# Values beside scores, a bank emptied ahead of a branch's end, and a gate product ahead of a scaling, in a three-block float32 transformer kernel

## The reference, cut to what matters

```
x = first_block(x, ...)     # two layers, each a mixer and a SwiGLU of width 2816
                            #   layer 0: short convolution and multiscale pooling
                            #   layer 1 ("block 1" below): sparse attention (8 heads of 64, 2 key groups;
                            #            selected + window + compressed branch) beside a 31-tap convolution
x = second_block(x, ...)    # "block 2"

# second_block
hn   = rms_norm(x)
qa,ka,va,ga, qb,kb,vb,gb, qc,kc,vc,gc, gate_logits = split(hn @ w_in)
o_a  = moba_attention(norm(qa), norm(ka), va)            # 8 heads
o_b  = dilated_attention(norm(qb), norm(kb), vb)         # 3 groups of 8 heads, merged by their log-sums
o_c  = swa_sink_attention(norm(qc), norm(kc), vc, sinks) # 8 heads, 2 key heads
branches = [o_a * silu(ga), o_b * silu(gb), o_c * silu(gc)]
br   = branches[i] @ w_branch[i]                         # i = 0, 1, 2
merged = sum(sigmoid(gate_logits[i]) * br[i])
x = x + merged @ w_out
```

## Time and profile before

| | |
|---|---|
| median of 3 runs | 994.49 us (994.39, 994.49, 996.18) |
| profiled execution | 996.31 us |
| its span, first to last instruction | 994.4 us |
| mean granted TensorE clock | 0.993 |
| TensorE busy | 972.7 us, 98% |
| VectorE busy | 608.2 us, 61% |
| ScalarE busy | 484.9 us, 49% |
| GpSimd busy | 213.2 us, 21% |
| HBM | 169 GB/s over the span |

### The profile page before, as it was taken

One profiled execution on the slowest core, in us unless ns is written; L12 is line 12 of the kernel. 1 busy time (PEld: TensorE's weight loads), 2 busy tenths in 40 slices (PEclk: granted clock), 3 DMA queues, 4 the chain that ended last, 5 costly groups with the idle time before them and its releaser, 6 DMA issues.

```text
span 994.4 us, 17117 instructions
## 1 busy us (share of the span) xinstructions
PE 972.7 (98%) x7057; PEld 867.0 (87%) x7057; DVE 608.2 (61%) x827; ACT 484.9 (49%) x726; POOL 213.2 (21%) x178
## 2 busy tenths in 40 slices
PE   9999999999998988999999999999999999999998
PEld 8989999999887877799999997887787888999996
DVE  5866554545488788665444446756464745856654
ACT  5446434343445364753343436456455545647451
POOL 0005970000032140000000000313543604920100
PEclk9999999999999999999999999999999999999999
DMA  8664656555557421356565663645354535553361
GB/s 267 219 217 143 216 175 205 170 199 180 179 158 238 134 99 44 127 180 202 171 208 169 204 218 128 212 169 170 127 170 165 174 129 170 170 189 111 127 211 43
DMA packets 119636, 168.75 MB, mean 170 GB/s; under 512 B 5556, under 2 KB 88596, under 8 KB 119572
## 3 DMA queue, kind: packets, MB, share of 16 engines
q1 hardware_dynamic: 118992, 167.55, 50.8%
q10 hardware_dynamic: 580, 0.30, 0.1%
HBM read 165.38 MB, written 2.46 MB: 169 GB/s over the span
## 4 chain that ended last, share of the span: by engine, by line
PE 84%; DVE 7%; ACT 3%; POOL 2%; issue 2%; SPq 1%; DMA 1%; DVEq 0%; ACTq 0%; POOLq 0%
PE ps L465 24%; PE ps L466 24%; PE ps L467 24%; PE ps L847 2%; DVE scratch_sb L1459 2%; PE ps L874 2%; PE ps L861 2%; DVE wlo_sb L445 1%; SPq L1268 1%; POOL b_inv_sb L2403 1%; PE ps L518 1%; PE ps L687 1%; PE ps L2027 1%; ACT whi_sb L422 1%; DVE nmax_sb L943 1%
## 5 line engine op out<-in xcount | busy, mean ns | idle before, releaser
L445 DVE TENSOR_TENSOR wlo_sb<-raw_sb,whi_sb 128x2048 fp32r<-128x2048 f32 x143 | 331.8, 2322 | 210.5 <-ACT whi_sb L422 210.2
L422 ACT ACTIVATE whi_sb<-raw_sb 128x2048 fp32r<-128x2048 f32 x143 | 273.8, 1916 | 186.2 <-PE ps L467 163.2
L465 PE MATMUL ps<-hhi_sb,whi_sb 128*128 128x256 f32 x1008 | 282.8, 281 | 1.7 <-ACT scratch_sb L2154 1.3
L467 PE MATMUL ps<-hhi_sb,wlo_sb 128*128 128x256 f32 x1008 | 281.4, 279 | 0.0
L466 PE MATMUL ps<-hlo_sb,whi_sb 128*128 128x256 f32 x1008 | 281.3, 279 | 0.0
L465 PEld LDWEIGHTS ps<-hhi_sb,whi_sb 128*128 128x128 f32 x1008 | 189.5, 188 | 4.1 <-issue 2.7
L466 PEld LDWEIGHTS ps<-hlo_sb,whi_sb 128*128 128x128 f32 x1008 | 189.4, 188 | 0.9
L467 PEld LDWEIGHTS ps<-hhi_sb,wlo_sb 128*128 128x128 f32 x1008 | 189.4, 188 | 0.0
L465 PE MATMUL ps<-whi_sb,hhi_sb 128*128 128x512 f32 (+2 forms) x304 | 121.1, 398 | 0.9 <-DVE wlo_sb L445 0.9
L466 PE MATMUL ps<-wlo_sb,hhi_sb 128*128 128x512 f32 (+2 forms) x304 | 117.9, 388 | 0.0
L467 PE MATMUL ps<-whi_sb,hlo_sb 128*128 128x512 f32 (+2 forms) x304 | 117.8, 388 | 0.0
(11 more groups left out here) (333 smaller groups left out, 1349.7 us busy)
## 6 DMA issues: line engine op xcount, KB each, us to landing
raw_sb<-w_in SPq DMA_DIRECT2D x45, 1024.0 KB, 5.0
raw_sb<-ffn_gate SPq DMA_DIRECT2D x22, 1024.0 KB, 5.1
raw_sb<-ffn_up SPq DMA_DIRECT2D x22, 1024.0 KB, 5.1
raw_sb<-ffn_down SPq DMA_DIRECT2D x22, 1024.0 KB, 4.8
raw_sb<-w_in_even SPq DMA_DIRECT2D x8, 1024.0 KB, 9.2
raw_sb<-w_in_odd SPq DMA_DIRECT2D x8, 1024.0 KB, 5.2
raw_sb<-w_branch SPq DMA_DIRECT2D x6, 1024.0 KB, 4.9
scratch_sb<-bias_rows_dram SPq DMA_DIRECT2D x40, 128.0 KB, 3.0
```

What stands on the lines that cost most here:

```text
L422: nc.scalar.activation(place(whi, n0), in_raw(n0), ACT.Copy).then_inc(hi_ready, 1)
L445: nc.vector.tensor_tensor(place(wlo, n0), in_raw(n0), place(whi, n0).bitcast(F32), ALU.subtract).then_inc(lo_ready, 1)
L465: nc.tensor.matmul(dst, l_hi, r_hi, start=first, stop=False)
L467: return nc.tensor.matmul(dst, l_lo, r_hi, start=False, stop=last)
```

## The change

It has five edits, all of them of order; no operation is added or removed.

- In block 2's `pe_step` the value products of the pairs before stand ahead of this step's transposes.
- In block 1 `VALUE_STEP` is 4, 8, ..., 32 instead of 6, 10, ..., 30, 32. Within a step TensorE's order is scores, transposes, values, so a value product now follows the scores of its step.
- In the segment of unit 3 the entry `finish` of branch 1 is taken out and put in behind the next `half`, which is the first half of the SiLU gate item of branch 2. On ScalarE the split of tile 34 and the emptying of that half come ahead of the exponential.
- VectorE's split of tile 46 (it stood behind the second part of tile 44, item R of branch 1) moves into `merge` (1, 1), behind its product.
- `scale_tile` of branch 2 for the first token half moves from the end of `finish2` to the same place: merge product, scaling and gating, split of tile 46, and only then the addition.

```diff
--- before.py
+++ after.py
@@ -965,12 +965,12 @@
             if 2 * m + 2 < len(jobs) // 2:
                 pair_s(pe, jobs, p0, 2 * m + 2)
                 pair_s(pe, jobs, p0, 2 * m + 3)
+            if m >= 1:
+                pair_pv(pe, jobs, p0, 2 * m - 2)
+                pair_pv(pe, jobs, p0, 2 * m - 1)
             if 0 <= 2 * m < len(jobs) // 2:
                 pair_t(pe, jobs, p0, 2 * m)
                 pair_t(pe, jobs, p0, 2 * m + 1)
-            if m >= 1:
-                pair_pv(pe, jobs, p0, 2 * m - 2)
-                pair_pv(pe, jobs, p0, 2 * m - 1)
 
         def dve_step(dve, jobs, p0, m):
             if 2 * m + 2 < len(jobs) // 2:
@@ -1011,7 +1011,7 @@
         GROUP_STEP, CONV3_REST, LATE_STEP = (10, 18, 26), 30, (10, 12, 14)
         STEPS1, FOUR_STEP = range(-2, 33), [-2, 0, 4, 8, 12, 16, 20, 24, 28, 32]
 
-        TURN_STEP, VALUE_STEP = range(1, 30, 4), [*range(6, 31, 4), 32]
+        TURN_STEP, VALUE_STEP = range(1, 30, 4), range(4, 33, 4)
 
         CONV3_AT = [0, 2, 4, 6, 8, 10, 12, 14, 16, 18, 20, 22, 25, 28, 31]
 
@@ -1924,6 +1924,9 @@
                         done = max(done, min(want, len(steps)))
                 assert done == len(steps)
                 body = mixed
+                if u == 3:
+                    k = body.index(("finish", 1))
+                    body.insert(next(j for j in range(k, len(body)) if body[j][0] == "half"), body.pop(k))
             if not order:
 
                 body[1], body[2] = body[2], body[1]
@@ -2232,7 +2235,8 @@
         def blk2_dve(dve):
             for e in order:
                 if e[0] == "weights" and e[4] == 1:
-                    split_lo(dve, e[2] + 2)
+                    if e[1][:3] != ("R", 1, 1):
+                        split_lo(dve, e[2] + 2)
                 elif e[0] == "sums":
                     _, item, nq = e
                     heads = 4 if item[0] == "kv" else 8
@@ -2276,6 +2280,9 @@
                             dve.wait_ge(b_T, LAST_Q_T)
                         nc.vector.scalar_tensor_tensor(mt[:, :, :], gs[:, :, :], 1.0, rb[:, :, :],
                                                        ALU.add, ALU.mult).then_inc(m_mul, 1)
+                        if (who, j) == (1, 1):
+                            scale_tile(dve, nc.vector, 2, 0, o_scaled, 0, FACTORS[2])
+                            split_lo(dve, n0 + 2)
                         dve.wait_ge(m_mul, 2 * who + j + 1)
                         nc.vector.tensor_tensor(macc[:, 4 * j:4 * j + 4, :], macc[:, 4 * j:4 * j + 4, :],
                                                 mt[:, :, :], ALU.add).then_inc(m_sum, 1)
@@ -2357,8 +2364,6 @@
                 step(nc.vector.tensor_tensor(comb[:, 3], comb[:, 3], comb[:, 2], ALU.add))
                 step(nc.vector.reciprocal(comb[:, 4], comb[:, 3]))
                 step(nc.vector.tensor_tensor(comb[:, 5], comb[:, 4], comb[:, 1], ALU.mult))
-            if b == 2:
-                scale_tile(dve, nc.vector, b, 0, o_scaled, 0, at)
 
 
         FACTORS = (2, 10, 17)
```

## The result

The changed kernel took 987.38 us (median of four executions, 986.99 to 989.07), the kernel before beside it 995.01 us (four, 994.39 to 996.18). The ratio is 0.9922, with a 95% interval of 0.9904 to 0.9939. It was run twice more, each time beside the kernel before: 990.25 us against 994.27 (ratio 0.9952, 0.9935 to 0.9968), and 988.04 against 994.44 (0.9932, 0.9915 to 0.9948). The three gains are 7.6, 4.0 and 6.4 us: each is clear of its interval, and the size differs. Both facts have to be explained.

A forecast was written before the change was run, and what follows sets the result against it. TensorE, busy 98% of the span, bounds the kernel; only its idle gaps, clock and gaps between instructions can give time. Terms -0.8 + 0.5 - 0.2 - 0.6 = -1.1 us take 994.49 to 993.4 us, range 989.7 to 995.8.

The forecast's parts named there:

- Part 2: Block 2's pe_step, value products ahead of transposes: a cost of 0.5 us, with the 1.89 us GpSimd wait staying.
- The same 0.08 us is a cost of each of the 15 steps: Block 2 steps holding both kinds: value products start later behind weights than transposes do, costing 0.4 to 1.2 us.
- which leaves 0.06. So this wait stays.: VectorE's copy at 693.17 comes only 0.06 us earlier, so TensorE's 1.89 us wait for GpSimd at 705.06 remains.
- Rival 1: Wait at 705.06 (1.89 us) and slow stretch behind it (1.7) go if sums come over 0.12 earlier: 989.8 us; chance 0.13.
- I cost this at nothing: Block 2, VectorE's score shifts (L886) come 0.6 or 1.1 us later in steps 1 and 2: no cost.
- rival 3: Block 2, turn of q2 at 737.92: a 1.5 us wait and a 1.7 us slow stretch, 996.6 us; chance 0.10.
- three signs of being wrong: Slow stretches other than four, GpSimd scalings changing length anywhere, or gaps around moved products not 0.1 us.
- Part 1: Block 1, values two steps earlier: output rows start sooner, gain 0.8 us, between 0.3 and 1.1.
- The delays ahead of it: Block 1, VectorE's chain held back by earlier value products: some 0.1 us, plus 0 to 0.5 us.
- Part 3: Block 2, finish 1 behind the next half: TensorE starts at 851.7 instead of 851.91, gain 0.2 us (0 to 0.4).
- Part 4: Branch 2's product at 940.36, gate product first on VectorE: gain 0.6 us of the 1.27 us wait.
- The slow stretches: TensorE at 1.2 GHz: four stretches of about 3.4 us in the trace, each costing at most 1.7 us.

The follow-up runs named there:

- e5: Kernel before, with value products ahead of transposes only in steps m = 1 and 2 of each block 2 attention unit: 994.82 us, ratio 0.9997.
- e2: Kernel before, with only block 1's VALUE_STEP changed to 4, 8, ..., 32: 993.49 us, ratio 0.9987.
- e3: Changed kernel with block 2's value-product order and block 1's VALUE_STEP turned back, leaving the finish move and the branch 2 edits: 993.22 us, ratio 0.9989.
- e4: Kernel before, with one added wait that sends VectorE's split of tile 15 behind GpSimd's scalings: 991.54 us, ratio 0.9971.
- e6: Kernel before, with value products ahead of transposes in one step alone, m = 3 of block 2's first unit: 991.38 us, ratio 0.997.
- f7: Changed kernel with transposes ahead of value products again in the third unit's step m = 2 alone: 988.43 us, ratio 0.9935.
- f9: Changed kernel with finish of branch 1 back ahead of the next half: 989.65 us, ratio 0.9953.
- h1: Changed kernel with finish of branch 1 back ahead of the half, and transposes first again in the fourth unit's step m = 2: 989.90 us, ratio 0.9951.
- a4: The whole changed kernel unaltered, run a third time beside the kernel before: 988.04 us against 994.44, ratio 0.9932.
- e1: Kernel before, with only block 2's value products put ahead of transposes in pe_step: 990.68 us, ratio 0.9965.
- f8: Changed kernel with block 1's VALUE_STEP as before: 990.33 us, ratio 0.9954.

## Why the prediction was wrong, by its own steps

**Part 2 is where it failed**, in two steps.

The first is "The same 0.08 us is a cost of each of the 15 steps". I had compared how late the first instruction of either kind starts behind weights, and left out what stands *between* the two kinds. Behind scores both kinds start alike. The timeline of before, in the first unit's m = 1, then the one of after:

```profile
677.48 0.28 PE L847 MATMUL ps<-qkh_sb,qkl_sb 64*128 64x128 f32 x2
677.70 1.09 PE L861 MATMUL ps<-ident_sb,scratch_sb 128*128 128x128 f32 x8
678.72 0.69 PE L874 MATMUL ps<-scratch_sb 128*64 128x64 f32 x16
```

```profile
674.14 0.28 PE L847 MATMUL ps<-qkh_sb,qkl_sb 64*128 64x128 f32 x2
674.36 0.69 PE L874 MATMUL ps<-scratch_sb 128*64 128x64 f32 x16
674.97 1.09 PE L861 MATMUL ps<-ident_sb,scratch_sb 128*128 128x128 f32 x8
```

The weight loads (engine PEld) that follow the eight transposes, in before and then in after:

```profile
678.72 0.55 PEld L874 LDWEIGHTS ps<-scratch_sb 128*64 128x64 f32 x16 [0.17 <-issue]
```

```profile
675.79 0.19 PEld L465 LDWEIGHTS ps<-whi_sb,hhi_sb 128*128 128x128 f32 x1
```

Eight transposes followed by value products take 678.72 - 677.70 = 1.02 us. Followed by weights they take less: 675.79 - 674.97 = 0.82 us. The value products take 0.61 us whichever comes next. So a value product behind transposes costs 0.20 us more than the next product's weights do, and the new order has no such pair. By the starts of the products themselves it is 0.17 us: the first weight product starts 0.85 us behind the transposes. The trace of before had it as an idle 0.17 us of the weight load ahead of these value products, which I did not read. Ten steps gain 0.2 each, as e5's lead shows one by one. The five steps without scores gain almost nothing (first unit: 2.34 us between the same two weight products, against 2.38).

The second is "which leaves 0.06. So this wait stays." Both numbers of that comparison were off. First the shift. VectorE's copy starts at 689.28:

```profile
689.28 1.29 DVE L894 COPY scratch_sb<-ps 128x512 f32<-128x512 f32 x2 [1.91 <-PE ps L861]
```

With the lead of 3.76 at that place this is 693.04 on the clock of before, where the copy stood at 693.17. That is 0.13 us earlier, not 0.06. I had started the sum from 691.80, the start that the chain of waits gives for the transposes; in the timeline they start at 691.64:

```profile
691.64 1.03 PE L861 MATMUL ps<-ident_sb,scratch_sb 128*128 128x128 f32 x8
```

The same sum from 691.64, with the 0.08 in it, gives 692.95, which is 0.22 us earlier. Two views differ by more than the margin that the sum was to decide.

Then the margin. I had it at 0.12 us (700.89 and 1.04 for the first scaling). The second scaling has its own row in the trace of before, and its start is 0.08 us behind the split's 701.81:

```profile
701.89 3.11 POOL L2411 TENSOR_TENSOR scratch_sb<-scratch_sb,b_inv_sb 128x512 f32<-128x512 f32 x1
```

In the changed kernel GpSimd's scalings go through (both, and then the second by itself), and VectorE's split behind them:

```profile
697.00 2.05 POOL L2416 TENSOR_TENSOR scratch_sb<-scratch_sb,b_inv_sb 128x512 f32<-128x512 f32 x2
```

```profile
698.00 1.04 POOL L2416 TENSOR_TENSOR scratch_sb<-scratch_sb,b_inv_sb 128x512 f32<-128x512 f32 x1
```

```profile
698.01 3.18 DVE L445 TENSOR_TENSOR wlo_sb<-raw_sb,whi_sb 128x2048 fp32r<-128x2048 f32 x1
```

Against the lead the scaling came 0.11 us earlier and the split 0.02, so the distance between them moved by 0.09 us, and 0.08 was enough. The second scaling now starts 0.01 us ahead of the split. All fourteen profiles follow this order of starts. In the four with the wait (before, e2, e3, e5) the split starts 0.07 to 0.08 us ahead and the second scaling takes 3.1 us. In nine of the others the scaling starts ahead by 0.02 us or less and takes 1.04; in e4 the added wait puts the split 1.13 us behind. The Trainium skill (SBUF — State Buffer, "Who interferes with whom") says that a VectorE instruction with two SBUF inputs and a GpSimd instruction that reads SBUF exclude each other for a whole instruction. The traces agree in both orders: scalings 4.12 us and split 2.29 before, 2.05 and 3.18 after.

**Rival 1 came true**, at a chance of 0.13. Its mechanism is the one that happened, and its threshold was not: it asked for over 0.12 us, and 0.09 did it. That a shift of 0.09 us met a margin of 0.08 is luck of this change. Rival 1 puts the time at 989.8; the measured 987.38 lies 2.4 lower, most of it the 0.5 us that I charged for the steps and the 1.4 net that they gave. Its price was 3.6 us, and 2.1 of it (the wait) came each time: 2.07 in the changed kernel (3.78 to 5.85), 2.10 in e6, 2.06 in e4. The other 1.5 us is the slow stretch behind the wait. It is looser than I wrote. Two of the four profiles with the wait have the stretch (before and e5), two don't (e2 and e3, here e2):

```profile
704.37 1.09 PE L2027 MATMUL ps<-ident_sb,scratch_sb 128*128 128x128 f32 x8 [1.89 <-POOL scratch_sb L2411]
```

```profile
706.00:707.00 1.00, 1.00 (x6) 0.82 (x5) 1.00 (x2) 1.00 (x2) 1.00 (x2) 1.00 1.04 408
```

None of the ten profiles without the wait has it. So no stretch stood there without the wait, and the wait did not always bring one.

"I cost this at nothing", on the later score shifts of VectorE, failed too, and at places that my rival 3 did not name. Transposes that stand 1.09 us later put softmax, query half and branch's end 1.09 later. Where the next turn had less slack than that, TensorE waits: 0.22 us, a lead lost by 0.35, at the third unit's end (f7 removes it), and 1.1 to 1.3 us in the fourth (f9 has it, h1 removes it). Rival 3 itself did not happen: at 737.92 there is no wait and the lead grows. Of the three signs of being wrong that the prediction gives, all came: other numbers of stretches, scalings of another length, and gaps of 0.2 us and not 0.1.

**Part 1** was right in mechanism and a little small: 0.8 forecast (0.3 to 1.1), 1.1 to 1.3 measured at equal slow stretches (0.7 to 1.5 between single profiles). At the end of block 1 the rows start 2.51 us after L1120 (389.30 less 386.79), against 3.74 in the earlier trace rows: 1.23 us, where I had 1.14. The idle 2.40 us of ScalarE is 0.29, and `ylo` starts as the last tap ends, with no idle time:

```profile
386.04 1.09 ACT L902 ACTIVATE scratch_sb<-ps 128x512 f32<-128x512 f32 x2 [0.29 <-PE ps L861]
```

```profile
388.52 0.68 DVE L1588 TENSOR_TENSOR ylo_sb<-ps,yhi_sb 128x512 fp32r<-128x512 f32 x1
```

The delays ahead of it were priced at 0.1 to 0.6 us. They can't be told from the scatter: at two stretches apart, the time from the first scores to L1120 is 54.82 to 55.24 us with the values early (e2, f7, a4) and 54.68 to 55.10 with the values at their old steps; at one stretch it is 53.45 (f9) against 53.53 and 53.52.

**Part 3** was forecast at 0.2 and gives nothing alone. What TensorE waits for at that place is the copy of the bank that its own tile fills last, and moving `finish` does not bring that forward (850.66 in e3, 850.68 in before). Beside Part 2 it is worth 1.25 to 1.34 us, since it takes the bank out from behind a branch's end that Part 2 makes late. I had costed the parts one by one and never asked what one of them would expose that another covers.

**Part 4** came to the size forecast, 0.6; L2154 is replaced by a wait of 0.54 us for `wlo`. Against e1, in which branch 2's product gains 0.22 from the last scores (910.00) on, the changed kernel gains 0.86, so 0.64. The size is in part luck. VectorE's product, the two of `scale_tile` and the split, and GpSimd's second operation beside them:

```profile
925.01 1.66 DVE L2281 SCALAR_TENSOR_TENSOR scratch_sb<-scratch_sb 128x1024 f32<-128x1024 f32 x1 [0.55 <-ACT scratch_sb L2164]
926.59 1.78 DVE L2382 TENSOR_TENSOR scratch_sb<-scratch_sb,comb_sb 128x512 f32<-128x512 f32 x1
928.41 0.69 DVE L2389 TENSOR_TENSOR scratch_sb<-scratch_sb 128x512 f32<-128x512 f32 x1
929.02 2.29 DVE L445 TENSOR_TENSOR wlo_sb<-raw_sb,whi_sb 128x2048 fp32r<-128x2048 f32 x1
```

```profile
925.67 2.16 POOL L2389 TENSOR_TENSOR scratch_sb<-scratch_sb 128x512 f32<-128x512 f32 x1
```

On the clock of before (lead 8.37) the split ends at 939.68, where the sum had 939.67. But the product is through at 935.04 and not at 936.18, and `scale_tile` then takes 2.43 us and not 1.2. The two errors cancel.

**The slow stretches.** I wrote that I am wrong if they number other than four. They do, but ahead of block 2 as scatter of either kernel, worth 1.0 to 1.4 us each by the executions. Within one kernel's executions, from two stretches to five, the time spans 4 us.

The sum of block 2, from the leads: 2.1 for the wait, 1.5 for the slow stretch that before had behind it, 0.6 for Part 4, and 1.4 net for the shorter steps (2.0 less the 0.35 of the third unit and some 0.2 elsewhere) are 5.6 of the 5.66 measured. Part 1 adds 1.1 to 1.3 in block 1. Together they are 6.7 to 6.9 against a before with the stretch at 705, and 5.2 to 5.4 against one with as many stretches as the changed kernel. The executions at equal clock say 5.7 to 6.0 (6.9 in the line of two and two), so about half a microsecond is not accounted for.

**Still open:** why the 34 us of matrix products ahead of the fifth unit are 0.3 us longer in some profiles (e3, e4, f7, f8, a4) with no wait in the trace; what decides how many slow stretches block 1 gets; what else scatters by up to 1.6 us ahead of block 1's attention; and what in TensorE makes the 0.20 us between transposes and value products.

## What to carry to other kernels

When two groups of instructions change places, cost every junction between kinds, as A to B, B to C and A to C, and not only the first start. Where a wait hangs on which of two engines takes the next turn, read the margin from one view, from the rows of the two instructions themselves, and count any shift near its size as one that can turn it and be worth microseconds; a wait added on the engine with slack can settle it, as e4 did. Cost the parts of a change also in pairs: the part that gains nothing alone may be the one that keeps another's gain.

## What the runs showed of the hardware that was not expected

- A float32 value product behind transposes starts 0.20 us later than a split weight product behind the same transposes (1.02 against 0.82 us after the first of eight, by the starts of the weight loads; 0.17 by the starts of the products).
- One exchange of 16 value products and 8 transposes moved a copy by 0.13 us and the kernel by 3.1 us (e6). An added wait gave 2.5 us (e4).
- Which of two instructions starts first, a VectorE split of 128 x 2048 or a GpSimd scaling of 128 x 512, goes with the scaling's length in all thirteen profiles without the added wait: 3.1 us where the split is 0.07 to 0.08 us ahead, 1.04 us where the scaling is ahead by 0.02 us or less.
- A slow stretch of the clock is not tied to the wait ahead of it: 2 of 4 profiles with the same 1.89 us wait at 704 to 705 us have one, 2 have none.
- The same code gets two to five slow stretches ahead of block 2 (its profiles show two, five and two). At the mean granted clocks that go with two and five, 0.997 and 0.991, it took 987.6 and 990.8 us.
